# Gathering tokens as quarter rows and turning them on VectorE in the experts' loop of a 32-expert layer

## The reference, cut to what matters

```python
def expert_block(args):
    xblk, e = args
    gu = xblk @ w_gu[e] + b_gu[e]
    gate, up = jnp.split(gu, 2, axis=-1)
    gate = jnp.minimum(gate, SWIGLU_LIMIT)
    up = jnp.clip(up, -SWIGLU_LIMIT, SWIGLU_LIMIT)
    act = (up + 1.0) * gate * jax.nn.sigmoid(SWIGLU_ALPHA * gate)
    return act @ w_down[e] + b_down[e]
```

## Time and profile before

| | |
|---|---|
| median of 3 runs | 2428.33 us (2425.53 to 2428.96) |
| the profiled execution | 2426.65 us |
| its span | 2424.6 us |
| the experts, from the first `onehot` to the end of the last `down` | 350 to 1460 us of the span |
| mean granted TensorE clock | 0.974 |
| read from memory, written | 535.8 MB, 25.0 MB |

### The profile page before, as it was taken

The page is one execution under the profiler, slowest core; times in us unless marked ns, Lnnn a source line. Parts: engine busy times, 40 slices in busy tenths (PEclk is TensorE's granted clock), DMA queues, the critical chain, the costliest instruction groups (busy, mean ns, idle before and its releaser), DMA issues. The chain is left out here.

```text
span 2424.6 us, 40637 instructions
## 1 busy us (share of the span) xinstructions
PE 2286.5 (94%) x17071; PEld 1023.0 (42%) x17071; DVE 686.2 (28%) x1189; ACT 494.4 (20%) x908; POOL 93.7 (4%) x105
## 2 busy tenths in 40 slices
PE   5999869999999999999999993799999998999998
PEld 2434433444444444444444441346445444444443
DVE  1133455111111111111111115102066202365633
ACT  2211222111110111111110111101016202355530
POOL 0000000000000000000000003000000000000000
PEclk9999989999999999999999995899999999999999
DMA  9148439999999999999999965321220121222100
GB/s 352 52 154 310 158 135 382 399 390 392 378 403 397 391 393 393 395 392 390 394 392 398 384 254 174 139 80 70 87 79 8 44 78 44 69 87 87 69 35 35
DMA packets 142024, 561.61 MB, mean 232 GB/s; under 512 B 16217, under 2 KB 31730, under 8 KB 108082
## 3 DMA queue, kind: packets, MB, share of 16 engines
q1 hardware_dynamic: 118662, 512.67, 54.7%
q0 software_dynamic: 9520, 35.26, 4.6%
q10 hardware_dynamic: 13788, 12.93, 1.6%
HBM read 535.77 MB, written 25.03 MB: 231 GB/s over the span
## 5 line engine op out<-in xcount | busy, mean ns | idle before, releaser
L1759 PE MATMUL ps<-ring,xeT 128*32 128x512 f32 x4096 | 491.2, 597 | 2.9 <-ACT xeT L1480 2.9
L1763 PE MATMUL ps<-ring,xeT 128*32 128x256 f32 x4096 | 268.7, 380 | 0.0
L1735 PE MATMUL ps<-ring,aT 128*32 128x512 f32 x2048 | 267.5, 594 | 1.1 <-DVE aT L1638 1.1
L1763 PEld LDWEIGHTS ps<-ring,xeT 128*32 128x32 f32 x4096 | 133.1, 110 | 199.0 <-issue 155.0
L1759 PEld LDWEIGHTS ps<-ring,xeT 128*32 128x32 f32 x4096 | 126.7, 110 | 197.0 <-issue 160.3
L1625 DVE TENSOR_SCALAR gate<-ps 128x768 f32<-128x768 f32 x32 | 30.6, 958 | 547.1 <-PE ps L1763 547.1
L1569 ACT ACTIVATE sig<-gate 128x768 f32<-128x768 f32 x32 | 27.0, 845 | 729.6 <-DVE gate L1625 729.6
L358 PE MATMUL ps<-hT_late,ring 128*128 128x512 f32 x384 | 165.2, 592 | 1.3 <-PEq L1999 1.3
L1740 PE MATMUL ps<-ring,aT 128*32 128x256 f32 x2048 | 157.6, 379 | 0.0
L1740 PEld LDWEIGHTS ps<-ring,aT 128*32 128x32 f32 x2048 | 67.0, 110 | 152.7 <-issue 152.7
L358 PEld LDWEIGHTS ps<-hT_late,ring 128*128 128x128 f32 x384 | 72.9, 190 | 92.9 <-issue 92.9
(11 more groups left out here) (371 smaller groups left out, 2190.0 us busy)
## 6 DMA issues: line engine op xcount, KB each, us to landing
ring<-in_w_gu SPq DMA_DIRECT2D x256, 1024.0 KB, 7.1
ring<-in_w_down SPq DMA_DIRECT2D x128, 1024.0 KB, 7.9
ring<-in_even_w_in SPq DMA_DIRECT2D x18, 1024.0 KB, 6.2
ring<-in_w_ada SPq DMA_DIRECT2D x32, 512.0 KB, 6.4
ring<-in_odd_w_in SPq DMA_DIRECT2D x32, 512.0 KB, 5.3
ring<-in_w_ada SPq DMA_DIRECT2D x8, 1024.0 KB, 21.0
ring<-in_w_in SPq DMA_DIRECT2D x8, 1024.0 KB, 15.8
y_scratch<-ysb ACTq DMA_DIRECT2D x128, 64.0 KB, 4.9
```

The lines of the kernel that those rows point to most:

```text
L1735: mm = nc.tensor.matmul(quad(Y0, 2 * q + n), acted(k, q), w[:, kk, n * BANK:(n + 1) * BANK], start=first, stop=last)
L1759: nc.tensor.matmul(quad(2 * b, 2 * q + h), left(q), w[:, at:at + BANK], start=start, stop=stop)
L1763: mm = nc.tensor.matmul(quad(2 * b + 1, c, 256), left(2), w[:, at:at + 256], start=start, stop=stop)
```

## The change

- `xe` is gathered by three indirect DMAs instead of one: gather q fetches the tokens 32q to 32q+31 of the expert as quarter rows of 1 KB, quarter i of a token to partition 32i + its number. Empty places get a row number out of bounds and are not fetched. The row numbers take six columns (`mine`) instead of two, a reduction and an addition.
- `xe` is turned by VectorE in 32 x 32 blocks (`dve_turn`) into `xturned` in SBUF; ScalarE modulates from there, 96 columns at a time. Modulation vectors in the new order (`mod2q`) are made once, by 16 small copies on ScalarE.
- A block of 32 partitions now holds one quarter of the features, so tile j of `w_gu` is made of rows 32j to 32j+31 of each quarter: `gu_pieces` loads four groups of 32 rows, 2 MB apart.
- `gate_up` is 12 matmuls of 512 columns instead of 8 of 512 and 8 of 256. The moving operand has runs of 32 columns (`part_columns`). Each PSUM bank 0 to 2 holds gate and up of 32 tokens.
- The activations are turned by VectorE from `up` into `aT` (`turned`) in one instruction, after the `down` of the step has read `aT`. All transposes on TensorE and the two copies from PSUM go away in the 32 experts.
- `pe_ids` stands at the end of a step, and writes bank 3. SP's loads after the first gather wait for all three gathers.

```diff
+        def gu_pieces(view, e, j):
+            return [(view, w_gu[e].rearrange("(q j f) n -> j q f n", q=4, j=KD)[j])]
...
-                    add(w_gu[e, j * P:(j + 1) * P, :], 2 * FF)
+                    stream.add(lambda view, e=e, j=j: gu_pieces(view, e, j), (2 * FF,))
...
         def pool_gather(pool, S):
-            nc.gpsimd.indirect_dma_start(xe[0:CAP, :], None, xn_dram, bass.IndirectOffsetOnAxis(ap=idx[0:CAP, :], axis=0)) \
-                .then_inc(S.gathered, 16)
+            for q in range(3):
+                nc.gpsimd.indirect_dma_start(xe[:, q * DQ:(q + 1) * DQ], None, quarter_rows,
+                                             bass.IndirectOffsetOnAxis(ap=idx[:, q:q + 1], axis=0),
+                                             bounds_check=4 * T - 1, oob_is_err=False).then_inc(S.gathered, 16)
+        def dve_turn(S):
+            nc.vector.transpose(xturned[:], xe[:]).then_inc(S.xT_done, 1)
...
         def act_modulate(act, S):
-            for k in range(KD):
-                nc.scalar.activation(xeT[:, k, :], ps[:, 6 + k // 4, (k % 4) * P:(k % 4 + 1) * P], ACT.Identity,
-                                     bias=mod2[:, k, 0:1], scale=mod2[:, KD + k, 0:1]).then_inc(S.xeT_read, 1)
+            for j in range(KD):
+                nc.scalar.activation(xeT[:, j, 0:CAP].rearrange("p (q s) -> p q s", q=3),
+                                     xturned[:].rearrange("p (q j s) -> p j q s", q=3, j=KD)[:, j], ACT.Identity,
+                                     bias=mod2q[:, 0, j:j + 1], scale=mod2q[:, 1, j:j + 1]).then_inc(S.xeT_read, 1)
...
         def dve_onehot(dve, S, place_, third_):
             for t in range(NT):
-                ins = nc.vector.tensor_scalar(onehot[:, t, 0:CAP], iota1[:, 0:CAP], pos(t), None, ALU.is_equal)
+                nc.vector.tensor_scalar(onehot[:, t, :], slots, place_(t), None, ALU.is_equal)
+                ins = nc.vector.scalar_tensor_tensor(out=mine[:, t, :], in0=cst[:, C_THIRD:C_THIRD + 6], scalar=third_(t),
+                                                     in1=tokens[:, t, :], op0=ALU.is_equal, op1=ALU.mult)
...
                     (SP's loop)
-                            src = w_gu[i + (1 + ahead), j * P:(j + 1) * P, :]
+                            [(dst, src)] = gu_pieces(view, i + (1 + ahead), j)
...
                     (VectorE, block_step)
-                    dve.wait_ge(M.gathered, e * 16 + 32)
-                    dve_ids(dve, M)
+                    dve.wait_ge(M.gathered, e * 48 + 96)
+                    dve_ids(dve, M, e + 3)
+                    dve.wait_ge(M.xeT_read, e * 8 + 8)
+                    dve_turn(M)
...
-                    dve.wait_ge(M.aT_done, e * 2 + 1)
-                    nc.vector.tensor_copy(turned[:, 0:BANK], bank(6)).then_inc(M.aT_read, 1)
-                    dve.wait_ge(M.aT_done, e * 2 + 2)
-                    nc.vector.tensor_copy(turned[:, Q2], bank(7, W - BANK)).then_inc(M.aT_read, 1)
+                    dve.wait_ge(M.act_ready, e + 1)
+                    if not first:
+                        dve.wait_ge(M.y_done, e * 2)
+                    nc.vector.transpose(turned[:, 0:W], up[:, 0:W]).then_inc(M.aT_read, 1)
...
                     (TensorE)
-                def gate_up(left, w, start, stop, done=None):
+                def gate_up(left, w, start, stop):
+                    for q in range(3):
                         for c in range(4):
+                            mm = nc.tensor.matmul(quad(q, c), left(q), part_columns(w, c), start=start, stop=stop)
...
                     pe.wait_ge(M.sel_ready, e + 1)
-                    gate_up(lambda q: sel[:, 0:QUAD], bparts, False, True, (M.gate_done, M.up_done))
-                    pe.wait_ge(M.gathered, e * 16 + 32)
-                    pe_turn(pe, M.xT_done, xe, first=stream.used)
+                    gate_up(lambda q: sel[:, 0:QUAD], bparts[:], False, True).then_inc(M.gate_done, 1)
                     if not first:
                         down(e, m0 + 8, turn)
-                    pe.wait_ge(M.act_ready, e + 1)
-                    pe.wait_ge(M.xeT_read, e * 8 + 16)
-                    pe_turn(pe, M.aT_done, up, first=None if first else stream.used, n=W // P)
+                    pe.wait_ge(M.onehot_ready, e + 4)
+                    pe.wait_ge(M.ids_read, e + 3)
+                    pe_ids(pe, M, first=stream.used)
```

More of the change, by code:

```diff
@@ L35 @@
 EPS = 1e-6
+NONE = 64 * P
 SLOTS, SLOT = 12, 2048
@@ L1441, in dve_sel, with pe_ids @@
         def dve_sel(dve, S, column):
             nc.vector.tensor_scalar(sel[:], ones[0:3 * E, :], column, None, ALU.mult).then_inc(S.sel_ready, 1)
-        def pe_ids(pe, S, settle=False):
+        def pe_ids(pe, S, first=None):
             for t in range(NT):
-                mm = nc.tensor.matmul(ps[:, Y0, 0:2], onehot[:, t, :], tokens[:, t, :],
+                mm = nc.tensor.matmul(ps[:, IDS, 0:6], onehot[:, t, :], mine[:, t, :],
                                       start=t == 0, stop=t == NT - 1)
+                if t == 0 and first:
+                    mm.then_inc(first, 1)
@@ L1448, in pe_ids, with pe_turn @@
             mm.then_inc(S.ids_done, 1)
-        def pe_turn(pe, signal_, src, first=None, n=KD):
-            for k in range(n):
+        def pe_turn(pe, signal_, src, first):
+            for k in range(KD):
                 mm = nc.tensor.transpose(ps[:, 6 + k // 4, (k % 4) * P:(k % 4 + 1) * P], src[:, k * P:(k + 1) * P], ident)
-                if k == 0 and first:
+                if k == 0:
                     mm.then_inc(first, 1)
-                if k % 4 == 3 or k == n - 1:
+                if k % 4 == 3:
@@ L1552, in _ @@
                 act.wait_ge(M.y_stored, 128)
+                for q in range(4):
+                    for m in range(4):
+                        parted.on(nc.scalar.copy(
+                            mod2q[q * QUAD:(q + 1) * QUAD].rearrange("p v (i m) -> p v m i", m=4)[:, :, m],
+                            mod2[m * QUAD:(m + 1) * QUAD].rearrange("p (v k) c -> p v k c", v=2)[:, :, 2 * q:2 * q + 2, 0]))
+                parted.wait(act)
                 act.wait_ge(bgu_loaded.sem, 48)
                 parted.on(nc.scalar.copy(bparts[:], bgu[:]))
-                act.wait_ge(M.xT_done, 2)
+                act.wait_ge(M.xT_done, 1)
                 act_modulate(act, M)
@@ L1597, in _, with list_step @@
             def _(dve):
-                rest.on(nc.vector.memset(onehot[:, :, CAP:], 0.0))
-                rest.on(nc.vector.tensor_copy(tokens[:].rearrange("p t c -> p (t c)"), cst[:, C_TOK:C_TOK + 2 * NT]))
+                def list_step(ins):
+                    listing.on(ins)
+                    listing.wait(dve)
+                split_places(list_step, posm[:], place[:], third_of[:])
+                for q in range(3):
+                    rest.on(nc.vector.tensor_copy(tokens[:, :, 2 * q:2 * q + 2],
+                                                  cst[:, C_TOK:C_TOK + 2 * NT].rearrange("p (t c) -> p t c", t=NT)))
                 rest.wait(dve)
@@ L1713, in tile @@
                     return view
-                for e in range(2):
+                for e in range(3):
                     pe.wait_ge(M.onehot_ready, e + 1)
@@ L1719, in _, with down @@
                     pe_ids(pe, M)
[L1720 to L1724, removed]
-                    pe.wait_ge(M.ids_read, e + 3 if not (isinstance(e, int) and e == E) else E + 2)
+                def down(e, m0, turn, final=False):
                     pe.wait_ge(M.y_read, e * 2)
-                    pe.wait_ge(M.aT_read, e * 2)
+                    pe.wait_ge(M.aT_read, e)
                     for j in range(4):
@@ L1736, in down @@
                                                       start=first, stop=last)
+                                if first and q == n == 0 and not final:
+                                    mm.then_inc(stream.used, 1)
                             if last:
@@ L1799, in _ @@
                     block_step(i + 1, 8, i, False)
-                down(E, 8 + 12 * (E - 1), 0)
+                down(E, 8 + 12 * (E - 1), 0, final=True)
                 stream.taken = end_moe
```

156 lines of the change are left out of this document (83 added, 73 removed).

## The result

| | us |
|---|---|
| before, median | 2428.28 |
| after, median of 4 runs | 4480.43 (4453.89 to 4485.06) |
| ratio, of the mean over six executions (these four, 4445.97 and 4481.45) | 1.8417, 95% interval 1.8335 to 1.8499 |
| the profiled execution after, its span | 4453.89, 4451.8 |

The changed kernel takes 84% longer. The profiled execution is the fastest of the four, 26 us under their median; what those 26 us are is not known. The page, to be held against the earlier trace rows: busy time and share, clock and DMA by slices, queues, one group of instructions.

The account below looks back on a forecast made before the run. TensorE was taken to bound the kernel before; after, four DMA engines at 92 us a step would end the experts near 3263 us, not 1460: 2426.65 + 1803 = 4230 us, range 2365 to 4400.

Parts of the forecast that it names:

- The likeliest case: Each w_gu tile loads on the same four DMA engines, which pace the experts: 4230 us, 4130 to 4400; chance 0.60.
- The step, 92 us: Four engines' time per expert: eight w_gu tiles at 10.0 us, four w_down at 2.55, gather and stores 2.2.
- The start, 361 us: End of the first gather, from which the remaining loads were counted; six early tiles had 85 us for the 60 needed.
- Loads on four engines: w_gu loads: the outer count of 4 groups sets 4 engines, the same each time; 3072 fewer queue packets, 115590.
- TensorE's turns, 1.73 us a step: Turns of xe and up leave TensorE: 1.83 us a step, 0.1 kept back for the row numbers' matmuls.
- Ahead of the first step, +3.5 us: Before the first expert matmul, small VectorE instructions, two more gathers and a turn add 3.5 us, between 2 and 6.
- VectorE's turn, 0.96 us: One turn on VectorE, estimated from a product of the same width: 0.96 us.
- Rival 1: w_gu loads use all 16 engines, or four different ones in turn; TensorE paces the kernel: 2375 us; chance 0.23.
- Rival 2: 16 engines become the bound in the experts at 33.4 to 34.1 us a step: 2390 to 2412 us; chance 0.11.
- Rival 3: Runs of 32 columns slow gate and up matmuls; 5% slower gives 2408 us; chance 0.06 shared with in-between engine counts.
- SP's queue hardly waits: Sign of four engines: SP's load queue, which waited 463 us for slots before, would hardly wait.
- A TensorE wait of 6 to 7 us at each tile: Sign of four engines: TensorE waits 6 to 7 us for each w_gu tile at the gate and up matmuls.

Follow-up runs that it names:

- experiments 7 and 9: Changed kernel with w_down tiles also grouped on four engines: 5139.47 us; changed kernel with w_gu tiles plain and only w_down grouped on four engines: 3791.55 us.
- experiment 2: Changed kernel with each w_gu tile loaded as 128 neighbouring rows, as before the change: 2360.25 us, 0.9724 of before.

## Why the prediction was wrong in size

The likeliest case came true in kind: four engines, the same for each tile, the packet count to the last packet, and a bound that has moved from TensorE to the loads. The DMA share in the experts was 0.42 at 134 GB/s, where I had written 0.35 to 0.4 at 145. The time is 4453.89 us in the profiled execution (median 4480) against 4230, outside even that case's own range to 4400. Taken at the end of the last `down`, 3263 was predicted and 3489.5 measured, 226 us. Two terms of the sum were too small and account for it.

- **The step, 92 us.** It measured 98.56. Its parts: a tile of `w_gu` on four engines 9.85 (10.0 predicted), gather and stores 0.5 (2.2), a tile of `w_down` 4.8 (2.55). The last one failed: 9.0 us a step too little, of which 2.9 came back by the other two (and the parts of my 92 add up to 92.4). I wrote that `w_down` "still uses all" engines and took its share at the rate it has alone, 411 GB/s; in fact grouped and plain loads together ran at 226 GB/s with all engines busy. The times of experiments 7 and 9 show that term: no plain tile, no loss; four in a step 9 us (4 x 2.3), eight at most 16 us (8 x 2.0). The 4.8 is what a tile of `w_down` costs in the sum, not how long its own packets take: a packet of `w_gu` takes 344 ns on average from 1000 to 2000 us against 311 where `w_gu` runs alone, and the 256 of them that an engine has in a step make 8.4 of the 9 us. 31 x 6.56 = 203 us.
- **The start, 361 us.** I took the six early tiles as issued long before and gave them 85 us. Three of them were issued that early; the others waited for slots and went out just ahead of the experts, and the small load of `b_gu` queued behind them on the four engines. SP and then ScalarE on the timeline:

```profile
339.79 1.66 SPq L165 DMA_DIRECT2D ring<-in_w_gu  x3
354.80 1.28 SPq L1552 DMA_DIRECT2D bgu<-in_b_gu  x3
368.67 10.59 SPq L1560 DMA_DIRECT2D ring<-in_w_gu  x3
```

```profile
383.11 1.90 ACT L1613 CAST bparts<-bgu 96x2048 bf16<-96x2048 f32 x1 [24.43 <-DMA bgu<-in_b_gu]
```

The last part of `b_gu` landed at 383.1, 27 us after its issue, where the three parts took 3.0 to 4.5 us before. Until then the four engines worked off what stood before it, so the stream of the experts began near 383 and not at 361: some 22 us. 203 + 22 = 225 of the 226 us. That the start is worth 22 is read from the trace; no run tried it alone.

By the other steps:

- *Loads on four engines.* Right. Against the 118662 of plain tiles, eight groups left out 118662 - 116614 = 2048 packets, eight for each of 256 tiles, 16 groups none: the number of engines is that of the groups. The Trainium skill ("DMA: Bandwidth & Descriptors", on why a DMA increments its semaphore by 16) has the same as a rule; by that rule, 4, 8 and 16 engines, the runs agree.
- *TensorE's turns, 1.73 us a step.* Measured where TensorE is the bound (experiment 2): 33.87 - 31.77 = 2.10. Beside the 1.83 of the turns, gate and up with bias and row numbers went from 21.75 us (20.99 + 0.76, the prediction's reading) to 21.47 (1319.92 to 1341.20, and 1351.63 to 1351.82); I had kept back 0.1 for the row numbers where 0.28 was gained.
- *Ahead of the first step, +3.5 us.* Right without the jam: in experiment 2 the first matmul of gate and up starts at 364.56 against 361.57, 3.0 later.
- *VectorE's turn, 0.96 us.* It takes 971 ns for `xturned` and 978 for `aT`.
- *Rival 1, 2375 us.* As a forecast it fell. As the time of 16 engines at full rate it can be held against the plain loads, which made 2360. 12 of the 15 us are the larger gain in a step (31 x 0.37); the clamp of the first step, 2.3 us later and not 3.5, is one more.
- *Rival 2, engines as the bound at 16.* It fell. The windows of experiment 2 show a share of 1.02 at 414 and 415 GB/s, where the earlier trace rows had 1.00 at 389 to 398; SP still waits 437 us, 214 times, for slots, against 463 in the earlier trace rows. A share of 1.00 had not been the end of what the engines could move.
- *Rival 3, runs of 32 columns.* It fell as well: 20.63 us for eight k steps in experiment 2.
- *SP's queue hardly waits.* Right: in its loop 18.0 us, twice, for gate and up matmuls.
- *A TensorE wait of 6 to 7 us at each tile.* 6.2 on average (1521.6 us, 247 times); 4.5 to 8.4 in the step shown, with a tile taking 4.1 to 5.4 us at the lower clock.

## What to carry to other kernels

Count what the outermost dimension of a load is on either side before you reorder its rows: four groups turned a 1 MB load on 16 engines into one on four, at the same bytes and the same data packets, and the first sign is the packet count of its queue. Don't mend it by splitting the load into bands of partitions; lay out the small operand (here four copies of 1.15 us) so that the large one stays a plain load of 128 partitions. When a load slows, look also at what is queued behind it on the same engines and at what runs beside it: a price taken from a stretch where one kind of load runs alone doesn't hold in a mix.

## What the runs showed of the hardware that I had not expected

- Engines can be busy all the time at about half their rate. 25 to 26 GB/s for each engine in plain loads of 128 partitions (415 GB/s, share 1.02) and in the four-engine loads alone (105 GB/s, 0.25); 14 in the mix of these two (226 GB/s, 0.99) and in loads of 32 partitions alone (224, 1.02). The DMA share alone doesn't tell these apart; it must be read with the GB/s beside it.
- With 16 groups and with eight, the same loads run at different rates within one execution: 395 and 229 GB/s at a share of 1.01 and 1.03, 194 and 128 GB/s at 0.51. It depends on more than the pattern; on what isn't known.
- For bands of 32 partitions the side that is written decides. Rows 64 KB apart ran at 415 GB/s into 128 partitions, neighbouring rows at 224 into bands of 32, and four DMAs a tile at 395 where each filled 128. For 16 groups it isn't shown.
- The Trainium skill ("SBUF — State Buffer", on Door 1, the DMA port swizzle) says that partitions 0 to 31 reach only 8 of 16 ports, some 218 GB/s, and all 128 reach every port. The 224 GB/s where only loads of 32 partitions move agree with that.
